# A two-block transformer layer: rows scaled on ScalarE and transposed in the second norm of block 2, and upper halves of weights multiplied first

## What is computed

```
def _rmsnorm(x, w):
    y = xf * lax.rsqrt(jnp.mean(xf * xf, axis=-1, keepdims=True) + NORM_EPS)
    return (y * w).astype(x.dtype)
...
        merged = jax.nn.sigmoid(ga) * y_a + jax.nn.sigmoid(gb) * y_r
        x = x + gate1 * jnp.dot(merged, w_out)

        h2 = _rmsnorm(x, norm2_w) * (1.0 + scale2) + shift2
        ffn = jnp.dot(jax.nn.silu(jnp.dot(h2, w_ffn_gate)) * jnp.dot(h2, w_ffn_up), w_ffn_down)
        x = x + gate2 * ffn
```

## Time and profile before

| | |
|---|---|
| median of 3 runs | 832.73 us (832.47 to 832.75) |
| the profiled execution, whole | 833.49 us |
| its span | 831.80 us |
| granted clock of TensorE, mean | 0.998 of full speed |
| TensorE products busy | 817.0 us, 98% of the span |
| VectorE busy | 600.7 us, 72% |
| ScalarE busy | 461.0 us, 55% |
| GpSimd busy | 60.4 us, 7% |

### The profile page before, as it was taken

The page is one execution under the profiler, slowest core; times in us unless marked ns, Lnnn a source line. Parts: engine busy times, 40 slices in busy tenths (PEclk is TensorE's granted clock), DMA queues, the critical chain, the costliest instruction groups (busy, mean ns, idle before and its releaser), DMA issues.

```text
span 831.8 us, 12284 instructions
## 1 busy us (share of the span) xinstructions
PE 817.0 (98%) x4255; PEld 680.3 (82%) x4255; DVE 600.7 (72%) x949; ACT 461.0 (55%) x744; POOL 60.4 (7%) x85
## 2 busy tenths in 40 slices
PE   8999999999999999999999999999999999999995
PEld 6887777898888888877977877888888888888884
DVE  5667757777888988878868997556666765566556
ACT  6547765466555556567644456545445554455443
POOL 3000000110111100300410000010000000000000
PEclk9999999999999999999999999999999999999999
DMA  9765445679999999543965574544652756655631
GB/s 292 275 187 169 126 129 154 231 286 392 358 329 323 334 326 330 195 129 83 280 202 147 174 216 135 169 152 152 179 177 76 227 182 211 198 168 180 213 111 50
DMA packets 88458, 171.53 MB, mean 206 GB/s; under 512 B 6448, under 2 KB 35864, under 8 KB 88416
## 3 DMA queue, kind: packets, MB, share of 16 engines
q1 hardware_dynamic: 82432, 142.56, 53.4%
q0 software_dynamic: 5824, 28.35, 9.9%
q10 hardware_dynamic: 160, 0.07, 0.0%
HBM read 168.84 MB, written 1.05 MB: 204 GB/s over the span
## 4 chain that ended last, share of the span: by engine, by line
PE 92%; DVE 4%; issue 1%; DMA 1%; ACT 1%; SPq 0%; POOL 0%; POOLq 0%; DVEq 0%; ACTq 0%
PE B L1594 20%; PE B L1596 20%; PE B L1595 20%; PE B L1632 15%; PE B L1637 8%; PE B L1715 2%; PE B L1745 2%; PE B L1723 1%; PE B L1736 1%; DVE w_lo L984 1%; DMA raw<-in_w_in_dram 1%; PE B L1619 0%; PE B L1617 0%; PE B L1618 0%; PE B L1969 0%
## 5 line engine op out<-in xcount | busy, mean ns | idle before, releaser
L1594 PE MATMUL B<-w_hi,xT 128*128 128x512 f32 (+3 forms) x584 | 228.7, 392 | 2.1 <-DVE w_lo L984 1.0
L984 DVE TENSOR_TENSOR w_lo<-raw,w_hi 128x1024 fp32r<-128x1024 f32 (+3 forms) x154 | 185.3, 1210 | 56.1 <-ACT w_hi L553 54.3
L1596 PE MATMUL B<-w_hi,xT 128*128 128x512 f32 (+3 forms) x584 | 223.3, 382 | 0.0
L1595 PE MATMUL B<-w_lo,xT 128*128 128x512 f32 (+3 forms) x584 | 223.0, 382 | 0.0
L553 ACT ACTIVATE w_hi<-raw 128x1024 fp32r<-128x1024 f32 (+3 forms) x154 | 157.5, 1030 | 90.8 <-PE B L1596 87.3
L1594 PEld LDWEIGHTS B<-w_hi,xT 128*128 128x128 f32 x584 | 109.8, 188 | 25.1 <-issue 3.0
L1596 PEld LDWEIGHTS B<-w_hi,xT 128*128 128x128 f32 x584 | 109.7, 188 | 21.7
L1595 PEld LDWEIGHTS B<-w_lo,xT 128*128 128x128 f32 x584 | 110.0, 188 | 19.2
L1558 DVE TENSOR_TENSOR w_lo<-raw,w_hi 128x1024 fp32r<-128x1024 f32 x60 | 71.4, 1220 | 28.2 <-ACT w_hi L951 28.2
L951 ACT ACTIVATE w_hi<-raw 128x1024 fp32r<-128x1024 f32 x60 | 62.1, 1055 | 40.0 <-PE B L1637 31.1
L1244 DVE TENSOR_TENSOR w_lo<-raw,w_hi 128x1024 fp32r<-128x1024 f32 x56 | 67.2, 1221 | 22.0 <-ACT w_hi L761 21.1
(11 more groups left out here) (224 smaller groups left out, 946.2 us busy)
## 6 DMA issues: line engine op xcount, KB each, us to landing
raw<-in_w_in_dram SPq DMA_DIRECT2D x79, 512.0 KB, 3.8
raw<-in_w_ff_dram SPq DMA_DIRECT2D x64, 512.0 KB, 7.7
Z<-in_w_ada_dram POOLq DMA_DIRECT2D x32, 768.0 KB, 7.8
raw<-in_w_ffn_gate_dram SPq DMA_DIRECT2D x44, 256.0 KB, 3.7
raw<-in_w_ffn_up_dram SPq DMA_DIRECT2D x44, 256.0 KB, 4.4
raw<-in_w_ffn_down_dram SPq DMA_DIRECT2D x20, 512.0 KB, 4.4
raw<-in_w_mix_out_dram SPq DMA_DIRECT2D x8, 512.0 KB, 3.8
raw<-in_w_ple_gate_dram SPq DMA_DIRECT2D x8, 512.0 KB, 4.4
```

The costliest lines, as they stand in the source:

```text
L984: nc.vector.tensor_tensor(w_lo[:, u % SPLIT, :, 0:n], raw[:, st.slot[u], :, 0:n], w_hi[:, u % SPLIT, :, 0:n].bitcast(F32), ALU.subtract).t ...
L1594: nc.tensor.matmul(bank, xh, wh, start=start, stop=False)
L1595: nc.tensor.matmul(bank, xh, wl, start=False, stop=False)
L1596: return nc.tensor.matmul(bank, xl, wh, start=False, stop=stop)
```

## The change

Two things. First, `unit_pair` waits for the unit's upper halves, does its eight products with them, then waits for the lower halves and does the four products with those; the wait for lower halves ahead of its calls is gone. Second, in the second norm of block 2 the diagonal and the products with it are replaced: ScalarE multiplies each half of a tile's rows by their roots into `nat` (`scale_rows`), and TensorE transposes the result by the identity, half by half (`scaled_rows_T`). For this ScalarE's order in the stage is written anew: the splits of U_FN to U_FN + 3 and tile 1's squares stand at other places between the modulations.

```
             for half in range(2):
                 squares(5, half, sem("h_done"), 13 + half, tiles=(0,))
+            split_to(U_FN)
+            scale_rows(0)
+            act.wait_ge(sem("mod_2"), 1)
+            modulate(4, 0, gate_a2, ada_col[:, 16:24], temp2, (0,))
+            squares(5, 0, sem("h_done"), 14, tiles=(1,))
+            modulate(4, 0, gate_a2, ada_col[:, 16:24], temp2, (1,))
             split_to(U_FN + 1)
-            squares(5, 0, sem("h_done"), 14, tiles=(1,))
-            act.wait_ge(sem("mod_2"), 1)
-            modulate(4, 0, gate_a2, ada_col[:, 16:24], temp2)
-            split_to(U_FN + 2)
             modulate(6, 4, gate_a2, ada_col[:, 16:24], temp2, (0,))
             squares(5, 1, sem("h_done"), 15, tiles=(1,))
             modulate(6, 4, gate_a2, ada_col[:, 16:24], temp2, (1,))
+            split_to(U_FN + 2)
+            scale_rows(1)
             split_to(U_FN + 3)
             modulate(5, 0, gate_a2, ada_col[:, 16:24], temp2)
             modulate(7, 4, gate_a2, ada_col[:, 16:24], temp2)
...
+            def scale_rows(t):
+                act.wait_ge(sem("rstd_done"), 6 + t)
+                for half in range(2):
+                    nc.scalar.activation(nat[:, half, t, :], h[:, t, 512 * half:512 * half + 512], ACT.Copy, scale=rstd[:, 5, t:t + 1])\
+                        .then_inc(sem("rows_scaled"), 1)
...
             mean_square_of(5, 0, 22)
-            scaled_identity(5, 6, (0,))
...
             split_modulated(0, 4, temp2, (1,))
-            scaled_identity(5, 7, (1,))
...
+                pe.wait_ge(hi_done, u + 1)
                 for kk in range(2):
                     for t in range(TILES):
-                        rows = slice(t * P, (t + 1) * P)
-                        m = mm3(B[:, banks[t], 0:n], xh[:, kt0 + kk, rows], xl[:, kt0 + kk, rows],
-                                w_hi[:, s, kk, 0:n], w_lo[:, s, kk, 0:n], first and kk == 0, last and kk == 1)
+                        o, rows = B[:, banks[t], 0:n], slice(t * P, (t + 1) * P)
+                        nc.tensor.matmul(o, xh[:, kt0 + kk, rows], w_hi[:, s, kk, 0:n], start=first and kk == 0, stop=False)
+                        nc.tensor.matmul(o, xl[:, kt0 + kk, rows], w_hi[:, s, kk, 0:n], start=False, stop=False)
+                pe.wait_ge(lo_done, u + 1)
+                for kk in range(2):
+                    for t in range(TILES):
+                        m = nc.tensor.matmul(B[:, banks[t], 0:n], xh[:, kt0 + kk, t * P:(t + 1) * P], w_lo[:, s, kk, 0:n], start=False,
+                                             stop=last and kk == 1)
                 m.then_inc(units_used, 1)
...
+            def scaled_rows_T(t, banks):
+                for half, b in enumerate(banks):
+                    pe.wait_ge(sem("rows_scaled"), 2 * t + half + 1)
+                    for k in range(4):
+                        m = nc.tensor.transpose(B[:, b, k * P:(k + 1) * P], nat[:, half, t, k * P:(k + 1) * P], ident)
+                    m.then_inc(sem("wt_done"), 1)
...
                     if t and i == 7:
-                        pe.wait_ge(sem("h_done"), 14)
-                        pe.wait_ge(sem("rstd_id"), 3)
-                        normed_rows(h, 0, (4, 6))
+                        scaled_rows_T(0, (4, 6))
...
                 if kp == 3:
-                    pe.wait_ge(sem("h_done"), 16)
-                    pe.wait_ge(sem("rstd_id"), 4)
-                    normed_rows(h, 1, (5, 7))
+                    scaled_rows_T(1, (5, 7))
```

More of the change, by code:

```diff
@@ L111 @@
     "affine": "DVE: modulated contraction tiles", "affine_lo": "DVE: lower halves of modulated pairs",
-    "squares": "ACT: sums of squares", "ms_done": "DVE: mean squares", "rstd_done": "Pool: rstd", "rstd_id": "DVE: diag(rstd), a tile of rows each",
+    "squares": "ACT: sums of squares", "ms_done": "DVE: mean squares", "rstd_done": "Pool: rstd", "rstd_id": "DVE: diag(rstd), a tile of rows each", "rows_scaled": "ACT: halves of a tile of rows times their root",
     "half_done": "DVE: rstd / 2", "nr8_done": "DVE: -rstd / 8", "h_done": "DVE: quarters of the residual",
@@ L1780, in _ @@
                     elif u:
-                        pe.wait_ge(lo_done, u + 1)
                         unit_pair(u, xT_hi, xT_lo, 2 * kp, banks, kp == 0, kp == 3)
@@ L1946, in _ @@
                 pe.wait_ge(sem("wt_lo"), 12 + (kp + 1 if kp else 2))
-                pe.wait_ge(lo_done, U_PG + kp + 1)
                 unit_pair(U_PG + kp, sT_hi, sT_lo, 2 * kp, (4, 5), kp == 0, kp == 3)
@@ L2073, in _ @@
                     pe.wait_ge(sem("wt_lo"), 20 + kp + 1)
-                pe.wait_ge(lo_done, U_WO + i + 1)
                 unit_pair(U_WO + i, sT_hi, sT_lo, 2 * kp, (4 + 2 * half, 5 + 2 * half), kp == 0, False)
```

## The result

The changed kernel took 833.88 us, the median of 22 runs (832.9 to 835.32), beside 832.98 us for the kernel before on the same chip (22 runs, 832.47 to 833.86). The ratio is 1.0013, with a 95% interval of 1.0008 to 1.0019. That is inside the 0.2% that I called no change, but it is on the other side of the forecast (832.5, a gain of 0.2), and 0.2 us beyond the range's upper end. The profiled execution took 833.83, its span 832.1. Five of the 22 executions lie together at 835.12 to 835.32, four of them with a mean granted clock of 0.993, which no execution of any other kernel here has; no profile caught one of them.

What follows compares the result with a forecast made beforehand. The prediction took TensorE, busy 98% of the span, to bound the kernel. From a median of 832.7 us, -0.7 at the start and +0.5 for the norm gave -0.2 and 832.5 us, range 831.4 to 833.7.

Steps and rivals of the forecast that it cites:

- Part 2: Second norm of block 2: scaling on ScalarE and plain transposes cost 0.5 us, though 1.7 us of TensorE work goes.
- bound of 1.0: Norm stage, upper bound of its cost: 1.0 us if each of some ten handovers takes 0.05 more.
- Part 1: `unit_pair`, upper halves first: unit 2 starts earlier and unit 3 about 17.71 instead of 18.49, a gain of 0.7 us.
- Order at zero: `unit_pair`: changing bank in the new order costs zero; upper bound 0.003 us for each of 1,000 upper products.
- waits inside a unit at zero: `unit_pair`: 125 mid-unit waits for lower halves cost zero, as in `unit_T2`, whose lower products follow without a gap.
- The scaled halves at 0.69 each on ScalarE: Norm of block 2: ScalarE scales each 128x512 half in 0.686 us, by a similar scaled copy, neighbours overlapping by 0.1.
- The late split and the pause: Norm stage: ScalarE splits U_FN + 2 only at 638.11, so TensorE waits about 2.4 us before the first pass's third unit.
- The sum: Whole kernel: -0.7 at the start plus 0.5 for the norm gives -0.2 us, forecast 832.5.
- (a): Rival, `unit_pair`: the products' order costs time, at 0.003 us on each of 1,000 upper products 835.5 us; chance 6%.
- (b): Rival: the norm's saved 1.7 us of TensorE work reaches the end, with unit 2's whole 1.2 us: 829.8; chance 6%.
- (c): Rival: the gain at the start is lost, or the norm costs its bound: 833.2 to 833.7 us; chance 20%.
- (d): Rival: the norm is neutral, ScalarE's chain being shorter: 832.1 us, or 831.6 with 1.2 at the start; chance 18%.

Runs made afterwards that it cites:

- order alone: Kernel before with the new order of the 12 products in `unit_pair`, the wait for lower halves left ahead of product 1: 833.07 us, ratio 1.0001.
- Part 2 alone: Kernel before with the changed norm and ScalarE order, `unit_pair` in its old order with its one wait: 834.1 us, ratio 1.0013.
- the late split alone: Kernel before with only ScalarE's third split (U_FN + 2) moved behind the second pair of modulations, diagonal and products kept: 835.31 us, ratio 1.0029.
- second set: The changed kernel timed again, unaltered, beside the kernel before on another chip, 11 executions: 833.14 us, ratio 1.0004.
- Part 1 alone: Kernel before with `unit_pair` as changed and the norm with its diagonal as before: 832.39 us, ratio 0.9992.
- third split earlier: Changed kernel with the split of U_FN + 2 moved ahead of tile 1's second squares: 832.78 us, ratio 0.9998 against the kernel before.

## Why the prediction was wrong

The step that failed is in Part 2: what TensorE's new pause of 2.4 us does to the products behind it. The prediction has the pause, but prices the products that follow it at full speed, so the term for the clock is zero, in the sum and in its bound of 1.0. Where the clock fell, those products took 0.88 us more in the change (a stage of 11.91 against 11.03), and Part 2, put at 0.5, cost 1.5 to 1.6. Its median alone was 1.1 more than before, with an interval from 0.3 to 1.8. This explains the miss in part: the two parts' medians, -0.63 and +1.1, give half of the +0.90, and the rest is open, as said below.

- *Part 1, -0.7.* Right in size, -0.63 with an interval from -1.4 to +0.1, and by the wait as far as the runs tell. In its steps it was partly luck. Unit 3 was to give back 0.4 of unit 2's 1.2 us by waiting for x's last tiles; of six profiles with Part 1, four show nothing there, the other two 0.1 and 0.2 us. And the wait that is saved isn't 1.0 us in each execution: in the five profiles of kernels with the old `unit_pair` it is 1.0, 0.8, 1.4, 0.6 and none. I took one execution's value for all.
- *Order at zero, waits inside a unit at zero.* Nothing speaks against it: the order alone gave 1.0001, and in the profile after, unit 2's lower products follow its upper ones at once (17.00, then 17.23).
- *The scaled halves at 0.69 each on ScalarE.* Right: two in 1.33 to 1.34 us.
- *The late split and the pause.* Right in place and size: 637.91 for the split against 638.11, a pause of 2.37 us where I said about 2.4. The second pass began at 642.67, 0.32 later on the clock than before, where I said 0.2 earlier; x came 0.86 later in this execution. At full clock Part 2 costs 0.58 by the profile, against my 0.5.
- *What the pause does.* Missed. I costed the products behind it at the duration that they had in a kernel whose longest wait there was 0.65 us. In 34 of 53 executions of the kernels that pause so, the mean clock shows a fall, and in the three profiles that caught it, the granted clock was half for about 3.4 us. The records that fall in it cost 0.88 us more in the change, 1.0 in Part 2 alone (12.05 less 11.02), and 1.6 in the late split with the old norm. My upper bound of 1.0 was made of handovers alone. The Trainium skill tells of such a fall in "TensorE: Matmul & The Clock Gate", section "HAM oscillation — how this bites in real kernels": work that follows a long wait of the array starts at the cold clock. The traces agree that it does (2.05 us for eight products that take 1.19 otherwise). The waits in that section of the Trainium skill are of about 3 to 5 us and bring it each time; here 2.4 us was enough, and in a part of the executions only.
- *The sum.* -0.05 at full clock and +0.83 at half. The first chip's +0.90 goes with 15 of 22 executions at a mean clock of 0.995 or less (median 834.1, the others 833.5), the second set's +0.32 with 4 of 11. Yet the first chip's three executions at 0.998 took 833.5, still 0.5 above before. The second set's seven at 0.996 and above were 0.1 above. That remainder of the first chip is open, and so are its five executions at 835.1 and above: the 0.993 of four of them is lower than in any profile with one such stretch (0.994 and 0.995). No run looked at either.
- *Rivals.* (a) is out by 1.0001, whose interval ends at 0.8 us more. (b) didn't come, but 0.69 of its 1.7 us is to be had once the split isn't late and tile 1's rows are scaled elsewhere. (c), 833.2 to 833.7, came nearest, for another reason: the start's gain wasn't lost by the run of Part 1 alone, and the handovers held (11.03 for a stage put at 10.92). (d), whose norm costs 0.1, doesn't fit the profiles: even at full clock the stage is 0.57 to 0.58 longer.

## What to carry to other kernels

When work is taken from the bounding engine and its helper's order is rewritten to do it, follow the helper's order to what it now delivers late: one moved split here outweighs 1.7 us of saved products. Put a price on each new pause of TensorE beyond its length: products behind a pause of over 2 us may run at half clock, and one profile may not show it, so look at the mean granted clock of all executions. Scale rows on the engine that is idle at that point, not on the one that is the chain.

## What the runs showed of the hardware

In three profiles the granted clock fell to half as a pause of TensorE of 2.4 us ended, or within 1 us behind it, and stayed there for about 3.4 us, in kernels otherwise 98% busy. A fourth profile has the same pause without the fall (the change's first, a granted clock of 1.0 throughout the stage). Over all executions, a mean clock of 0.995 or less came in 34 of 53 of the three kernels with the pause (the change 15 of 22 and 4 of 11, Part 2 alone 8 of 11, the late split alone 7 of 9), in none of 77 of the seven other changed kernels, and in none of 85 of the kernel before in these sets. With nine products of ones in the pause, 2.21 us of busy time, none of 33 executions of three kernels had it.

The 34 are a lower count. The mean also takes in the end of the span, where TensorE is idle: from 820 us on the granted clock was 0.70 in the change's first profile and 0.81 in that of the third split earlier, which moves the mean about as much as the stretch at half clock does. So a mean of 0.996 can stand for either.

Scaling 128x512 fp32 values by row from SBUF to SBUF, two in a row, took 1.33 us on ScalarE and 0.88 us on VectorE.
